# Hyena filters of a hybrid diffusion trunk: network on two partition halves, middle rows copied once, absolute values summed once per group

## What is computed

```python
hid = jnp.sin(fr * (z @ w1 + b1))
hid = jnp.sin(fr * (hid @ w2 + b2))
filt = (hid @ w3).reshape(length, 2, HYENA_ORDER, D_HYENA)
filt = filt * window[:, None, None, :]
fwd, bwd = filt[:, 0], filt[:, 1]
two_sided = jnp.concatenate([fwd, zeros, bwd[1:][::-1]], axis=0)
two_sided = two_sided / jnp.sum(jnp.abs(two_sided), axis=0, keepdims=True)
return jnp.fft.rfft(two_sided, axis=0)
```

## Time and profile before

| | us |
|---|---|
| median of 3 runs (3412.28 to 3417.86) | 3416.4 |
| the profiled execution, its own time | 3407.46 |
| its span, first to last instruction | 3405.7 |
| PE busy | 3194.1 (94%) |
| DVE busy | 2196.7 (65%) |
| ACT busy | 1655.7 (49%) |
| POOL busy | 373.3 (11%) |

### The profile page before, as it was taken

The page is one execution under the profiler, slowest core; times in us unless marked ns, Lnnn a source line. Parts: engine busy times, 40 slices in busy tenths (PEclk is TensorE's granted clock), DMA queues, the critical chain, the costliest instruction groups (busy, mean ns, idle before and its releaser), DMA issues.

```text
span 3405.7 us, 54105 instructions
## 1 busy us (share of the span) xinstructions
PE 3194.1 (94%) x22270; PEld 2430.2 (71%) x22270; DVE 2196.7 (65%) x2820; ACT 1655.7 (49%) x2154; POOL 373.3 (11%) x316
## 2 busy tenths in 40 slices
PE   4898999979899894999999999999999999999996
PEld 2443788878778773777777777777777777777774
DVE  6643333167666547777777777777777777777775
ACT  1102322156412333666666666666666666666663
POOL 1210100011244131000000000000000000000010
PEclk8999999989999896999999999999999999999998
DMA  3465342254676434788778778777777777777785
GB/s 138 182 221 195 99 128 94 72 146 126 223 245 218 150 101 165 278 299 293 273 289 298 274 285 295 275 288 289 278 289 281 281 291 280 285 283 289 277 325 200
DMA packets 226034, 791.14 MB, mean 232 GB/s; under 512 B 28525, under 2 KB 35321, under 8 KB 221564
## 3 DMA queue, kind: packets, MB, share of 16 engines
q1 hardware_dynamic: 206028, 722.02, 57.3%
q0 software_dynamic: 19760, 65.65, 6.7%
HBM read 730.31 MB, written 57.26 MB: 231 GB/s over the span
## 4 chain that ended last, share of the span: by engine, by line
PE 58%; DMA 1%; DVE 1%; ACT 0%; issue 0%; POOL 0%; SPq 0%; ACTq 0%; POOLq 0%; DVEq 0%
PE exp_bank L2779 15%; PE exp_bank L2781 14%; PE exp_bank L2780 14%; PE exp_bank L2789 14%; PE exp_bank L2761 1%; DMA out_y<-exp_xb 1%; PE exp_bank L2763 1%; DMA exp_xb<-residual 0%; PE exp_bank L2747 0%; DVE g_pick L2342 0%; DVE g_pick L2341 0%; DVE g_pick L2344 0%; DVE exp_lo L2475 0%; DMA exp_xq<-hidden_rows,g_rows_q 0%; PE exp_bank L2751 0%
## 5 line engine op out<-in xcount | busy, mean ns | idle before, releaser
L2475 DVE TENSOR_TENSOR exp_lo<-exp_raw,exp_hi 128x1024 fp32r<-128x1024 f32 x1056 | 1277.4, 1223 | 249.4 <-ACT exp_hi L2471 191.0
L2471 ACT ACTIVATE exp_hi<-exp_raw 128x1024 fp32r<-128x1024 f32 x1056 | 1119.2, 1061 | 572.0 <-PE exp_bank L2781 558.4
L2779 PE MATMUL exp_bank<-exp_hi,exp_xt 128*128 128x512 f32 (+1 forms) x1536 | 588.6, 383 | 1.3 <-DVE exp_xt L2628 1.0
L2781 PE MATMUL exp_bank<-exp_hi,exp_xt 128*128 128x512 f32 (+1 forms) x1536 | 571.9, 372 | 0.0
L2780 PE MATMUL exp_bank<-exp_lo,exp_xt 128*128 128x512 f32 (+1 forms) x1536 | 571.4, 372 | 0.0
L2779 PEld LDWEIGHTS exp_bank<-exp_hi,exp_xt 128*128 128x128 f32 x1536 | 289.4, 188 | 86.9 <-issue 39.1
L2781 PEld LDWEIGHTS exp_bank<-exp_hi,exp_xt 128*128 128x128 f32 x1536 | 289.6, 189 | 52.0
L2789 PE MATMUL exp_bank<-exp_raw,exp_xtp 128*32 128x256 f32 (+1 forms) x6144 | 324.1, 363 | 0.0
L2780 PEld LDWEIGHTS exp_bank<-exp_lo,exp_xt 128*128 128x128 f32 x1536 | 290.2, 189 | 45.4
L2779 PE MATMUL exp_bank<-exp_hi,exp_hid 128*128 128x512 f32 x704 | 283.7, 403 | 10.4 <-DVE exp_lo L2475 10.4
L2781 PE MATMUL exp_bank<-exp_hi,exp_hid 128*128 128x512 f32 x704 | 275.8, 392 | 0.0
(11 more groups left out here) (407 smaller groups left out, 4294.0 us busy)
## 6 DMA issues: line engine op xcount, KB each, us to landing
exp_raw<-in_w SPq DMA_DIRECT2D x1056, 512.0 KB
hy_table<-in_basis_s POOLq DMA_DIRECT2D x64, 512.0 KB
carry_tiles<-in_w_ada SPq DMA_DIRECT2D x24, 1024.0 KB, 5.6
proj_raw<-in_w_in SPq DMA_DIRECT2D x24, 512.0 KB
filt_table<-in_kbasis_s SPq DMA_DIRECT2D x18, 512.0 KB, 6.3
spectrum_s<-filt_spec SPq DMA_DIRECT2D x34, 256.0 KB, 2.4
carry_flex<-spectrum_s SPq DMA_DIRECT2D x16, 512.0 KB
features<-proj_xr SPq DMA_DIRECT2D x12, 512.0 KB, 3.0
```

The source lines that it names most:

```text
L2471: act.activation(st.hi[:, n % st.ns, :], raw(n), ACT.Copy).then_inc(st.hi_done, 1)
L2475: dve.tensor_tensor(st.lo[:, n % st.ns, :], raw(n), st.hi[:, n % st.ns, :].bitcast(F32), ALU.subtract).then_inc(st.lo_done, 1)
L2779: pe.matmul(out, xh, wh, start=(k == 0), stop=False)
L2781: mm = pe.matmul(out, xl, wh, start=False, stop=(k == nk - 1))
```

## The change

- *Network.* The 1024 sample columns stand as 512 columns on two halves of the partitions, in both layers; `w2` is loaded twice below itself, and the first layer's two matmuls write the two halves of one bank. Sin of the second layer goes back to 64 partitions in two steps. PE, DVE and ACT wait for the six loads that they need (`s_net`, `s_cond`) and for the others later. The sums of w3 and the low part of `W2` move from DVE to POOL, the zero half of `W2` to ACT.
- *Middle sample.* The two one-row matmuls of each such job go. Once, behind `gen(2)`, eight fp32 matmuls (`middle_rows`) spread the four rows with their signs over all partitions, ACT copies each result into `spread`, and DVE (`fold`) multiplies it by the inverse norm and adds the skip term; `spectrum_out` adds it in its second instruction, which odd sines now have too.
- *Absolute values.* For t > 0 POOL adds `MA` to `totals`, and PE runs `sums` once for each group (four times instead of ten). `sums(4)` and `close(1)` move behind the first job of the first loop.
- *Ada.* The steps that stood in the network go behind `gen(0)`, `gen(1)` and `close(0)` on PE, and behind `unit(0)` and `unit(1)` on DVE. Loads of w_ada and windows are placed differently.

The diff, cut:

```diff
-    SUM_AT = {2: 5, 5: 6, 8: 7, 11: 8, 14: 9}
+    SUM_AT = {2: 5, 14: 9}
...
+        totals = [opnd[:, 7, 0:2, :], opnd[:, 0, 0:2, :]]
...
@@ sync
-            ada(3)
-            sp.wait_ge(s_sin, 4)
+            sp.wait_ge(s_sin, 5)
...
-            for n in range(2, PER):
+            for n in range(2, PER - 1):
                 win_load(n)
-                if n < PER - 1:
-                    ada()
+                ada()
+            ada()
             basis_load(3)
+            ada()
+            win_load(PER - 1)
+            ada()
@@ tensor
+            def hidden_s(layer):
+
+                for h in range(2):
+                    rows, out = slice(64 * h, 64 * h + 64), pf[1 + layer][64 * h:64 * h + 64, :]
                     if layer:
-                        pe.wait_ge(s_sin, 1 if b == 0 else 2)
...
+                        pe.wait_ge(s_sin, 2)
+                        mm = pe.matmul(out, w2[rows], hid[rows, ZS:ZS + 512], start=True, stop=True)
+                    else:
+                        mm = pe.matmul(out, w1[:], z[:, ZS + 512 * h:ZS + 512 * h + 512], start=True, stop=True)
...
+            def middle_rows():
+                pe.wait_ge(s_mf, 4)
+                for k in range(8):
+                    gi, x = divmod(k, 2)
+                    if k >= 2:
+                        pe.wait_ge(s_spo, k - 1)
+                    pe.matmul(pk[k % 2][:], sgn[ones_at(gi), :], midf[ones_at(gi), x, :], start=True, stop=True).then_inc(s_sp, 1)
...
-                if rank1:
-                    gi, s = 2 * o + q, int(kind == "sin")
-                    pe.matmul(pk[n % 2][:], sgn[ones_at(gi), :], mid_h[ones_at(gi), s, :], start=False, stop=False)
-                    mm = pe.matmul(pk[n % 2][:], sgn[ones_at(gi), :], mid_l[ones_at(gi), s, :], start=False, stop=True)
...
-            hidden(0, (0, 1, 2))
-            ada(2)
-            hidden(1, (0,))
-            hidden(1, (1, 2))
+            pe.wait_ge(s_net, 16 * 6)
+            hidden_p(0)
+            hidden_s(0)
+            hidden_p(1)
+            hidden_s(1)
+            pe.wait_ge(s_in, 16 * 9)
+            gen(0)
             ada()
-            gen(0)
             gen(1)
+            ada()
             sums(0)
             middles()
             close(0)
-            ada()
+            ada(2)
             gen(2)
-            sums(1)
+            middle_rows()
             ada()
             for j in range(NJ[0]):
                 spectrum(0, 0, j)
             gen(3)
-            sums(2)
             ada()
             gen(4)
-            sums(3)
             ada()
-            sums(4)
-            close(1)
             for j in range(NJ[1]):
                 spectrum(0, 1, j)
+                if j == 0:
+                    sums(4)
+                    close(1)
@@ scalar
             absolute(0)
             absolute(1)
-            act.wait_ge(s_mf, 4)
-            act.activation(mid_h[:], midf[:], ACT.Copy).then_inc(s_mh, 1)
+            for k in range(8):
+                act.wait_ge(s_sp, k + 1)
+                act.activation(spread[:, k // 2, k % 2, :], pk[k % 2][:], ACT.Copy).then_inc(s_spo, 1)
             for n in range(2, len(UNITS)):
                 absolute(n)
@@ gpsimd
+            pool.wait_ge(s_w3, 32)
+            pool.tensor_tensor(wsum[:, :, 0, :], w3[:, 0], w3[:, 1], ALU.add).then_inc(s_ws, 1)
+            pool.tensor_tensor(wsum[:, :, 1, :], w3[:, 1], w3[:, 0], ALU.subtract).then_inc(s_ws, 1)
+            pool.wait_ge(s_wh, 1)
+            pool.tensor_tensor(W2[0:64], wsum[0:64], W1[0:64].bitcast(F32), ALU.subtract).then_inc(s_wl, 1)
...
+                if added(n):
+                    pool.wait_ge(s_MA, n + 1)
+                    if adds(n) % (MT - 1) != 1:
+                        pool.wait_ge(s_acc, adds(n) - 1)
+                    pool.tensor_tensor(totals[UNITS[n][0]], totals[UNITS[n][0]], MA, ALU.add).then_inc(s_acc, 1)
@@ vector
+            def fold(gi):
+                if gi == 0:
+                    dve.wait_ge(s_skip, 32)
+                dve.wait_ge(s_rn, gi + 1)
+                dve.wait_ge(s_spo, 2 * gi + 2)
+                dve.tensor_tensor(spread[:, gi, 0, :], spread[:, gi, 0, :], rn[:, gi, :], ALU.mult).then_inc(s_fold, 1)
+                dve.tensor_tensor(spread[:, gi, 1, :], spread[:, gi, 1, :], rn[:, gi, :], ALU.mult).then_inc(s_fold, 1)
+                dve.wait_ge(s_fold, 3 * gi + 1)
+                dve.tensor_tensor(spread[:, gi, 0, :], spread[:, gi, 0, :], skip[:, gi // 2, :], ALU.add).then_inc(s_fold, 1)
...
-            ada(2)
-            reduced(1, 0)
-            reduced(1, 1)
...
-            ada()
-            dve.wait_ge(s_wl, 2)
...
             unit(0)
+            ada()
             unit(1)
+            ada()
...
             inverse(0)
             ada()
             unit(2)
             ada()
+            fold(0)
             for j in range(NJ[0]):
                 spectrum_out(0, 0, j)
             unit(3)
```

More of the change, by code:

```diff
@@ L970, in summed @@
         def summed(eng, o, q, j):
-            silent = [closes(x, y) and not with_middle(x, y) for x in range(2) for y in range(NJ[x])]
+            silent = [closes(x, y) for x in range(2) for y in range(NJ[x])]
             n = q * NJ[0] + j
@@ L977, in summed, with added, adds @@
                 eng.wait_ge(s_k, (o * sum(NJ) + n + 1) - o * sum(silent) - sum(silent[:n + 1]))
+        def added(n):
+            return UNITS[n][1] > 0
+        def adds(n):
+            return sum(added(m) for m in range(n + 1))
         def ones_at(gi):
@@ L1099, in _, with hidden_p @@
             ada = Ada(ada_step)
[L1101 to L1107 removed]
+            def hidden_p(layer):
+                if layer:
+                    pe.wait_ge(s_sin, 1)
+                pe.matmul(pf[0][0:64, 0:ZS - ZP], w2[0:64] if layer else w1[:], (hid[0:64] if layer else z)[:, ZP:ZS],
+                          start=True, stop=True).then_inc(s_h, 1)
+            def hidden_s(layer):
+                for h in range(2):
+                    rows, out = slice(64 * h, 64 * h + 64), pf[1 + layer][64 * h:64 * h + 64, :]
+                    if layer:
+                        pe.wait_ge(s_sin, 2)
+                        mm = pe.matmul(out, w2[rows], hid[rows, ZS:ZS + 512], start=True, stop=True)
+                    else:
+                        mm = pe.matmul(out, w1[:], z[:, ZS + 512 * h:ZS + 512 * h + 512], start=True, stop=True)
+                mm.then_inc(s_h, 1)
             def gen(n):
@@ L1135, in sums @@
                 gi = group(n)
-                first = n == 0 or group(n - 1) != gi
-                pe.wait_ge(s_MA, n + 1)
-                if first and gi:
+                if UNITS[n][1] < 0:
+                    src = MA
+                    pe.wait_ge(s_MA, n + 1)
+                else:
+                    src = totals[UNITS[n][0]]
+                    pe.wait_ge(s_acc, adds(n))
+                if gi:
                     pe.wait_ge(s_rn, gi)
                 for m in range(2):
-                    mm = pe.matmul(pn[:], g["ones"][:], MA[:, m, :], start=(first and m == 0), stop=False)
+                    mm = pe.matmul(pn[:], g["ones"][:], src[:, m, :], start=(m == 0), stop=False)
                 mm.then_inc(s_sum, 1)
@@ L1250, in absolute @@
                     if n:
-                        act.wait_ge(s_sum, n)
                         act.wait_ge(s_MA, n)
+                        if UNITS[n - 1][1] < 0:
+                            act.wait_ge(s_sum, 1 if n == 1 else 3)
+                        elif added(n - 1):
+                            act.wait_ge(s_acc, adds(n - 1))
                     else:
-                        act.wait_ge(s_hl, 2)
+                        act.wait_ge(s_hl, 3)
                         act.wait_ge(s_AB, 2)
@@ L1310, in reduced @@
             def reduced(layer, part):
-                c0, c1 = ((ZP, ZS), (ZS, ZN))[part]
-                np_ = 128 if layer else 64
-                for b in ((0,) if part == 0 else (1, 2)):
-                    b0, b1 = BLK[b]
-                    dve.wait_ge(s_h, 3 * layer + b + 1)
-                    ins = dve.tensor_scalar(y[0:np_, b0:b1], pf[b][0:np_, 0:b1 - b0], fb[0:np_, layer:layer + 1],
-                                            fb[0:np_, 2:3], ALU.add, ALU.mult)
-                chain(ins)
-                if layer == 0 and part == 0:
-                    dve.wait_ge(s_h, 3)
-                yy, kx = y[0:np_, c0:c1], kk[0:np_, c0:c1]
+                np_, c0, c1 = ((64, ZP, ZS), (128, ZS, ZS + 512))[part]
+                bank = pf[1 + layer if part else 0]
+                yy, kx = y[0:np_, c0:c1], kk[0:np_, c0:c1]
+                dve.wait_ge(s_h, 2 * layer + part + 1)
+                if layer:
+                    dve.wait_ge(s_sin, part + 1)
+                else:
+                    dve.wait_ge(s_h, 2)
+                chain(dve.tensor_scalar(yy, bank[0:np_, 0:c1 - c0], fb[0:np_, layer:layer + 1], fb[0:np_, 2:3], ALU.add, ALU.mult))
```

120 lines of the change are left out of this document (65 added, 55 removed).

## The result

The kernel with the change takes 3490.1 us (median of 6 runs, 3482.6 to 3493.0), beside 3413.3 us for the kernel before, run with it (6 runs): ratio 1.022 [1.0207, 1.0234], slower by 77 us. Its profiled execution took 3482.61 us with a span of 3480.8; the one of before took 3407.46 with 3405.7. So 75.1 us of span are to be found.

The account below looks back on a forecast made before the run. PE was taken to bound the loops, a DVE-ACT-DVE chain the network; -14 + 17.7 + 2.9 + 54.8 + 3.6 + 12 - 3.5 = +73.5 us gave 3481 profiled, forecast 3490, range 3454 to 3528 (forecast's own 3462 to 3515).

Parts of the forecast that it names:

- The term that decided: First loop: PE, one ada step ahead, waits for DVE's copies, 49.5 us; with clock loss and work changes +54.8 us.
- Network: Network stage ahead of the loops: unit(0) begins at 34.2 instead of 48.24, a gain of 14 us.
- Middle stretch: From unit(0) to the first short job: middle rows on PE and eight ACT copies delay it, +17.7 us.
- From there to the first sample job: Stretch after the first short job, through gen(3), unit(3), gen(4) and unit(4): +2.9 us.
- The two serial steps: Two ada steps between the short jobs and the second loop become fully serial: +3.6 us.
- Second loop: Jobs 0 to 6: periods become 6.7 and 7.5 us instead of 4.94 and 5.79, +12 us at full clock.
- Its last part: Second loop, j = 8 to 16: five pairs gone, 4.3 us, part of it behind stores of spectra: -3.5 us.
- rival 1: Second loop: PE stays at 1.2 GHz because of its rests, 33 us more, 3523 us; chance 0.10.
- rival 2: POOL's add for six units holds up the next absolute, +15 us, 3505 us; chance 0.06.
- Rival 3: Copies are ready when PE comes, so only work counts: -28 us, 3388 us; chance 0.05.
- Rival 4: Seventeen later waits cost only their direct part, 36 us, units and inverses staying hidden: 3424 us; chance 0.05.
- The premise on the later phases: Every phase ends in a barrier of all engines, so the filters phase's gain or loss reaches the end undiminished.

Follow-up runs that it names:

- s6: Changed kernel with six ada calls each on PE and DVE, absolute(2) before the copies, POOL's adds on DVE, sums(4) and close(1) ahead of the loop: 3413.6 us.
- s3: Changed kernel with six ada calls each on PE and DVE, absolute(2) before the eight copies, and the old sums per unit on PE: 3399.6 us.
- s1: Changed kernel with only the new network and loads kept, old middle rank-1 pairs and old sums, six ada calls each on PE and DVE: 3400.3 us.
- s2: As s1, but the two sums of w3 and the low part of W2 moved from POOL back to DVE: 3396.2 us.
- e1_aligned: Changed kernel with one more ada call in DVE's list behind unit(2), so PE and DVE have seven each ahead of the first loop: 3419.65 us.

## Why the prediction was right, and where it was not

**The term that decided.** The waits of PE for the copy in the first loop were predicted from the two lists and the prices of the steps, as 11.2, 13.6, 1.6, 2.9, 6.3, 2.4, 3.7 and 7.8 us; they are 10.3, 12.7, 1.3, 5.2, 6.3, 2.2, 6.3 and 7.4. The two that are clearly too low, 2.9 for 5.2 and 3.7 for 6.3, lack DVE's own waits of 2.24 and 2.39 us for the window loads of units 7 and 9; 11.2 and 13.6 were too high. The clock was put at 18 us in this loop: PE is busy 7.2 us more, with 12.8 removed and 2.7 moved in, so 17.3. The loop costs 57.1 us where the sum had 54.8. (The terms as written add up to 54.4, and the 3 us of "today's own waits" are 1.8 by the earlier trace rows.) The experiments confirm the cause, not only the size.

**The other terms.** Network: -14 and -14.8; inside it two errors cancel. POOL's lock was taken at 5.3 us of the chain and costs DVE 7.3, while the chain without it, drawn to 28.9, comes out at 26.1 (33.41 less 7.3). Middle stretch: +17.7 and +19.3; the middle rows take 10.2 us instead of 7 to 8.4, `absolute(2)` does stand behind the eight copies (DVE rests 10.63 us for it), and the fold meets POOL's add (2.60 us for a step of 0.69). From there to the first sample job the sum had +2.9 and it is -0.9. The part from `gen(3)` on, 19.3 us before, was put at 24.9 and takes 23.7; the short jobs ahead of it, 13.4 us before, were put at 10.7 and take 8.0, as DVE waits 1.49 and 0.60 us for their stores where it waited 4.16. The two serial steps: +3.6 and +3.3. Second loop: +12 at full clock; it is 11 by the periods at the higher clock, and 14.4 with job 0, job 5 and the last ada step at the lower one. Its last part: -3.5 and -0.7; job 7 begins at the lower clock, and jobs 7 and 8 take 8.9 us instead of 7.0.

The sum of all, 73.5, stands against 77.5 at the end of the phase and 75.1 in the span. That the median came out at 3490.1 with 3490 forecast is closer than the terms are, and luck: the stretches were 4.0 us too low together, the later phases gave 2.4 back, and the median lies 7.5 above the profiled execution where 9 was taken. The forecast's own range does not follow from its terms either: a clock loss of 0 with a network gain of 19.3 gives 3467, not 3462, and 25 with 10 gives 3501, so that 14 us of the 3515 rest on the slower stores, for which no number was worked out.

**The rivals.** The clock (rival 1) is out: behind rests of 1.3 and 2.2 us five of the seven jobs of the second loop take 3.70 us, the others 5.05 and 5.40, and the loop costs 14.4 us more, where this rival had 33 on top of the 12. POOL as the bound (rival 2) doesn't show in the first loop of the kernel after, where PE's rests are all the copy's; with those gone the new sums cost 11 to 19 us, about the +15 that I had written. The number is near by luck: taking the adds off POOL (s6) brings only 4.6 us of it back. I had it as an alternative to the waits, and what there is of it was hidden beneath them. Rival 3 is where the judgement of the change itself was wrong. It said that with the copies ready in time the kernel comes to 3388, -28 us, because only work would count; the run that makes them ready gives 3419.65. The step that failed is "-15.4 pairs, -8.5 sums": PE's work removed was counted as time removed, one for one, while much of it was paid for by work on DVE, POOL or ACT that PE then waits for. s3 has none of the pairs in its first loop, 7.7 us less work, and the loop is 2.2 us shorter (98.2 for 100.4 in s1): PE rests 3.8 us instead of 1.7, and is busy only 4.4 us less, at a granted clock of 0.97 instead of 1.00. The pairs bring their share only where nothing new waits: from the second order's short jobs to the projection, with twelve pairs or 10.2 us less work, s3 is 9.6 us shorter than s1, which pays back the 9.1 us that the middle rows cost ahead of the loop. Rival 4 is out: the eight waits of the first loop alone are 51.7 us, and it had 36 for all seventeen.

**The premise on the later phases.** I wrote that what this phase gains or loses goes to the end undiminished. For the change it does, within 2.4 us. It is not exact: s2 ends the phase 19.3 us earlier than before and its span is 12.1 shorter. Of that 6.8 us are in the attention phase (table by stretches, of before and of s2):

```profile
695.59:900.24 204.65, 185.60 (x1385) 164.57 (x1385) 148.56 (x468) 127.65 (x268) 26.76 (x21) 0.96 0.46 132
```

```profile
678.94:890.36 211.42, 188.33 (x1384) 167.21 (x1385) 148.48 (x467) 127.52 (x268) 26.79 (x21) 0.94 0.45 127
```

The same code, at a granted clock of 0.94 for 0.96. Over the fourteen profiled kernels what lies behind `filters` takes 3078 to 3088 us. Whether it is the moment at which a phase begins that decides, or chance of one execution, no run here tells.

## What to carry to other kernels

When two engines walk through one sequence of small steps, each waiting for the other's last one, count the calls on each side ahead of every loop: a step moved on one list and not on the other costs nothing at its own place, and can cost a wait at every later step. Work taken off the busiest engine is a gain only if what replaces it is off that engine's waits, and if the work did not stand where the engine has to wait anyway: read which instruction will be the last to arrive at its next one, and on whose list it stands. And when a large loss has been explained, take its cause away and measure again; what lay beneath it here was a small loss where a gain was expected.

## What the chip showed that was not expected

- *A POOL instruction can hold a DVE step until it ends, also a step with one input.* I had taken two-input steps for the ones that suffer. The tensor_scalar of 512 columns took 2.26, 2.45 and 3.84 us beside POOL and 0.43 without it, and each of the three ended 0.3 us behind POOL's. Not every step is held: the tensor_scalar that reads PSUM (L1368) took 0.81 us at 22.30, inside POOL's 4.60 us, and 0.80 in s2 with POOL at rest. The Trainium skill (SBUF — State Buffer, "SBUF: two separate sides") says that a DVE operation in a mode with two ports, or with two inputs in SBUF, and a GpSimd operation exclude each other for a whole instruction. The rows agree with it.
- *The price of a rest is paid behind it.* The eight instructions of a job take 3.70 us at 2.4 GHz, 0.43 us from one to the next; at 1.2 GHz it is 0.86. Behind the rest of 5.30 us in e1_aligned the job took 6.21, behind those of 2.17 and 1.31 us in the second loop five jobs of seven took 3.70. In the first loop after the change the lower clock (0.81) added 17.3 us to 51.7 us of rest, a third on top.
